# A hybrid decoder layer on one core: expert routing and the last chunk's normalisation rearranged

## The reference

```python
y = mixer(x, ...)
x = layer_norm(ALPHA * x + y, ln1_w, ln1_b)
y = moe(x, router_w, router_b, w_gate, w_up, w_down)
x = layer_norm(ALPHA * x + y, ln2_w, ln2_b)

def moe(x, ...):
    s = sigmoid(x @ router_w)                       # 1024 tokens x 16 experts
    sel = s + router_b
    # the group (of 4 experts) with the greatest sum of its two best sel wins;
    # the two best experts of that group are taken
    gate = s of the two / their sum
    out = sum over e of combine[:, e] * ((silu(x @ w_gate[e]) * (x @ w_up[e])) @ w_down[e])
```

## Time and profile before

| | us |
|---|---|
| median of 3 runs (lowest, highest) | 1000.78 (1000.57, 1002.73) |
| the profiled execution's own time | 1001.21 |
| its span | 999.5 |
| TensorE busy in it | 909.5 |
| VectorE busy | 646.9 |
| ScalarE busy | 447.3 |
| GpSimd busy | 193.7 |
| mean granted TensorE clock | 0.956 of full |

### The profile page before, as it was taken

One profiled execution on the slowest core, in us unless ns is written; L12 is line 12 of the kernel. 1 busy time (PEld: TensorE's weight loads), 2 busy tenths in 40 slices (PEclk: granted clock), 3 DMA queues, 4 the chain that ended last, 5 costly groups with the idle time before them and its releaser, 6 DMA issues.

```text
span 999.5 us, 15243 instructions
## 1 busy us (share of the span) xinstructions
PE 909.5 (91%) x5056; PEld 781.3 (78%) x5056; DVE 646.9 (65%) x985; ACT 447.3 (45%) x586; POOL 193.7 (19%) x192
## 2 busy tenths in 40 slices
PE   6999999999985989998249999999999999999936
PEld 6998887888764878887249889898898988988911
DVE  3442699894236687785682668577689975243766
ACT  3531101102157334411423678576789966255513
POOL 3100011011121121100021322332234422214310
PEclk9999999999996999999559999999999999999969
DMA  7620213133516255312765869979699997648254
GB/s 280 214 90 1 95 52 127 55 125 107 179 63 209 81 184 168 121 64 106 294 206 182 307 201 365 357 249 372 185 373 392 393 373 266 188 120 258 43 183 174
DMA packets 70116, 194.91 MB, mean 195 GB/s; under 512 B 6990, under 2 KB 20640, under 8 KB 70080
## 3 DMA queue, kind: packets, MB, share of 16 engines
q1 hardware_dynamic: 58896, 156.36, 42.7%
q0 software_dynamic: 11040, 37.95, 14.0%
q10 hardware_dynamic: 144, 0.14, 0.0%
HBM read 158.75 MB, written 35.67 MB: 195 GB/s over the span
## 4 chain that ended last, share of the span: by engine, by line
PE 82%; DVE 9%; issue 5%; DMA 2%; ACT 1%; DVEq 0%; SPq 0%; POOL 0%; ACTq 0%; POOLq 0%
PE banks L1109 18%; PE banks L623 14%; PE banks L612 13%; PE banks L637 13%; PE banks L1106 9%; PE banks L1223 6%; PE banks L596 2%; PE banks L1244 2%; PE banks L603 1%; DVE arena L897 1%; DVE small L893 1%; PE banks L1090 1%; DMA sum_scratch<-work,tile_sums 1%; PE banks L1158 1%; DMA arena<-in_x 1%
## 5 line engine op out<-in xcount | busy, mean ns | idle before, releaser
L832 DVE TENSOR_TENSOR split_weights<-arena,split_weights 128x1024 fp32r<-128x1024 f32 x192 | 223.2, 1217 | 0.0
L670 ACT ACTIVATE split_weights<-arena 128x1024 fp32r<-128x1024 f32 x192 | 191.4, 1057 | 3.3 <-DMA arena<-in_w_up 1.8
L1109 PE MATMUL banks<-split_weights 128*128 128x512 f32 (+2 forms) x960 | 181.8, 350 | 0.0
L1109 PEld LDWEIGHTS banks<-split_weights 128*128 128x128 f32 x960 | 155.5, 190 | 23.9 <-issue 1.4
L623 PE MATMUL banks<-split_weights,split_rows 128*128 128x256 f32 x1152 | 147.5, 284 | 0.0
L623 PEld LDWEIGHTS banks<-split_weights,split_rows 128*128 128x128 f32 x1152 | 142.7, 191 | 1.9
L612 PE MATMUL banks<-split_weights,split_rows 128*128 128x512 f32 x576 | 137.4, 395 | 5.5 <-DVE split_rows L836 5.5
L637 PE MATMUL banks<-split_weights,split_hidden 128*128 128x512 f32 x576 | 137.5, 394 | 0.0
L612 PEld LDWEIGHTS banks<-split_weights,split_rows 128*128 128x128 f32 x576 | 110.1, 191 | 29.0 <-issue 5.9
L637 PEld LDWEIGHTS banks<-split_weights,split_hidden 128*128 128x128 f32 x576 | 106.5, 188 | 21.6
L554 POOL DMA_INDIRECT sum_scratch<-work,tile_sums x24 | 90.6, 3775 | 117.3 <-ACT work L707 105.0
(11 more groups left out here) (312 smaller groups left out, 996.2 us busy)
## 6 DMA issues: line engine op xcount, KB each, us to landing
arena<-in_w_gate SPq DMA_DIRECT2D x64, 512.0 KB, 7.7
arena<-in_w_up SPq DMA_DIRECT2D x64, 512.0 KB, 8.4
arena<-in_w_down SPq DMA_DIRECT2D x64, 512.0 KB, 10.4
arena<-in_w_in SPq DMA_DIRECT2D x20, 512.0 KB, 5.4
arena<-in_x SPq DMA_DIRECT2D x16, 512.0 KB, 6.3
arena<-in_w_out SPq DMA_DIRECT2D x8, 512.0 KB, 4.6
x_scratch<-arena SPq DMA_DIRECT2D x8, 512.0 KB, 2.9
sum_scratch<-arena SPq DMA_DIRECT2D x8, 512.0 KB, 4.4
```

The lines of the kernel that those rows point to most:

```text
L670: act.activation(unit_split(u, 0), unit_slot(u), AF.Copy).then_inc(xw_hi, 1)
L832: dve.tensor_tensor(unit_split(u, 1), unit_slot(u), unit_split(u, 0).bitcast(F32), ALU.subtract).then_inc(xw_lo, 1)
L1109: last = pe.matmul(b[:, 0:width], xT[:, hx, k, j * P:(j + 1) * P], wc[:, hw, k, 0:width], start=(k == 0 and i == 0), stop=(k == KC - 1 and ...
```

## The change

1. **Normalisation.** Statistics of a chunk's first half are taken one step earlier. The two passes `norm1` and the product with the weight become one centring pass (mean and weight, no square root needed) and one pass that scales and adds the bias. For the last chunk this second pass, the transposes of x1, their copy and the routing run in two halves. The x1 transposes read contiguous columns, and the router's weights are loaded in the order to match (pieces of 64 B instead of 512 B).
2. **First tile.** A short way gives its tokens: tile 0 holds expert 0's first 128 tokens, so the rank alone places them; a 128x1024 one-hot and 8 products of two columns give the token indices, and the gather of tile 0 starts at once. Its rows are transposed, copied and subtracted in halves. The list of all tokens is summed after that.
3. **Gates.** Normalised gates of all tokens and experts (64 B a token) are stored to DRAM once. For each tile GpSimd gathers the rows of its tokens, and ScalarE's scale is that row's column of the expert. Gate parts, gate one-hots and gate sums are gone.
4. **Weights.** Units 0 to 3 of the first expert are loaded in step 6 and split in steps 8 (2, 3) and 9 (0, 1); units 4 to 7 are loaded in step 7. The other units are split behind the rows. Two small constants are made in step 8.
5. Tile counts have a signal of their own, on which each engine waits before it reads them. In step 9 chunk 6's logits are read after the last chunk's centring pass. The final sums' loads use the staging semaphores.

```diff
 def sp_experts(sp):
-    sp.wait_ge(hT_ps, T)
-    for u in range(8):
-        load_unit(sp, 0, u)
...
+    sp.wait_ge(gates_ready, 1)
+    sp.dma_start(gate_dram[P:P + SEQ, :].rearrange("(t p) e -> p t e", p=P), rt[:, 2]).then_inc(gates_out, 16)
...
+    def gather_gates(j, first=False):
+
+        if not first:
+            pool.wait_ge(gate_in, 16 * j)
+        pool.tensor_copy(tok_gate, tok[:, bass.ds(j, 1)]).then_inc(gate_idx_ready, 1)
+        wait_apart(pool, gate_idx_ready, j + 1)
+        pool.indirect_dma_start(out=gate_rows, out_offset=None, in_=gate_dram,
+                                in_offset=bass.IndirectOffsetOnAxis(ap=tok_gate, axis=0)).then_inc(gate_in, 16)
...
+        if more or not last:
+            gather_gates(g + 1)
...
+    pool.wait_ge(first_tok_ready, 1)
+    pool.indirect_dma_start(out=xe, out_offset=None, in_=x1_dram,
+                            in_offset=bass.IndirectOffsetOnAxis(ap=tok1, axis=0)).then_inc(xe_in, 16)
     pool.wait_ge(tok_ready, 1)
-    gather(0, True)
     gather(1)
+    pool.wait_ge(gates_out, 16)
+    gather_gates(0, True)
     for i, src in enumerate((ln2_w[0], ln2_b[0])):
...
+    pe.wait_ge(first_hot_ready, 1)
+    for t in range(T):
+        last = pe.matmul(bank(3)[:, 0:2], hot_first[:, t, :], first_ids[:, t, :], start=(t == 0), stop=(t == T - 1))
+    last.then_inc(first_ps, 1)
...
+    pe.wait_ge(xe_in, 16)
+    for k in range(KC):
+        last = pe.transpose(psum[:, 4 + k // 4, (k % 4) * P:(k % 4 + 1) * P], xe[:, k:D:KC], ident[:, :])
+        if k == KC // 2 - 1:
+            last.then_inc(first_T, 1)
...
+    pe.wait_ge(ntiles_ready, 1)
+    pe.wait_ge(xw_lo, 4)
...
-    for u in range(8):
+    for u in range(4, UNITS):
...
+    for half, transposed, signal in ((0, first_T, first_hi), (1, xeT_ps, xe_hi)):
+        act.wait_ge(transposed, 1)
+        act.activation(XR[:, 0, half * 4:half * 4 + 4, :], bank(4 + half).rearrange("p (k n) -> p k n", n=P), AF.Copy).then_inc(signal, 1)
...
+        act.wait_ge(gate_in, g * 16 + 16)
         act.activation(ys, psum[:, 2:4, :].rearrange("p a n -> p (a n)"), AF.Copy,
-                       scale=gate_slot[:, bass.ds(g, 1)]).then_inc(y_sb, 1)
+                       scale=gate_rows[:, bass.ds(e, 1)]).then_inc(y_sb, 1)
...
-    dve.tensor_copy(ones_bf, ones[:, :])
-    dve.tensor_tensor(stri, tri[:, :], ident[:, :], ALU.subtract)
...
+    dve.wait_ge(dispatch_ready, 1)
+    own.link(dve.tensor_scalar(others, disp[:, :, 0], -1024.0, 1024.0, ALU.mult, ALU.add))
+    dve.tensor_copy(first_ids[:, :, 0], i_tok.to_broadcast([P, T]))
+    dve.tensor_copy(first_ids[:, :, 1], i_lo[:, 1:T + 1])
...
+    own.link(dve.tensor_tensor(first_key, bank(0)[:, 0:T * NE].rearrange("p (t e) -> p t e", t=T)[:, :, 0], others, ALU.add))
+    dve.tensor_tensor(hot_first, i_lo.unsqueeze(1).to_broadcast([P, T, P]), over(first_key, P), ALU.is_equal).then_inc(first_hot_ready, 1)
     own.link(dve.tensor_copy(cnt[:, 0, :], bank(1)[:, 0:NE]))
+    dve.wait_ge(first_ps, 1)
+    own.link(dve.tensor_copy(first_sum, bank(3)[:, 0:2]))
+    dve.scalar_tensor_tensor(tok1, first_sum[:, 1:2], float(P), first_sum[:, 0:1], ALU.mult, ALU.add).then_inc(first_tok_ready, 1)
+
+    own.link(dve.tensor_tensor(rtv(2), rtv(0), disp, ALU.mult))
+    own.link(dve.tensor_reduce(mx, rtv(2), AX.X, ALU.add))
+    own.link(dve.reciprocal(mx, mx))
+    dve.scalar_tensor_tensor(rtv(2), rtv(2), 1.0 / ALPHA, over(mx, NE), ALU.mult, ALU.mult).then_inc(gates_ready, 1)
...
-    dve.tensor_copy(ntiles[0:1, 0:2], packed_sum)
-    dve.tensor_scalar(ntiles[0:1, 2:3], cnt[0:1, 3, NE - 1:NE], 1.0 / P, None, ALU.mult)
+    dve.tensor_copy(ntiles[0:1, 0:2], packed_sum).then_inc(ntiles_ready, 1)
...
+    for half, copied, signal in ((0, first_hi, first_lo), (1, xe_hi, xe_lo)):
+        dve.wait_ge(copied, 1)
+        dve.tensor_tensor(XR[:, 1, half * 4:half * 4 + 4, :], bank(4 + half).rearrange("p (k n) -> p k n", n=P),
+                          XR[:, 0, half * 4:half * 4 + 4, :].bitcast(F32), ALU.subtract).then_inc(signal, 1)
...
-    of_both(gatew, 0)
...
-    for i in range(3):
-        last = dve.tensor_tensor(hot_gate[:, :, i * 32:(i + 1) * 32], hot_tile,
-                                 gate_parts[:, i].unsqueeze(2).to_broadcast([P, 2 * T, 32]), ALU.mult)
-    last.then_inc(gate_hot_ready, 1)
...
-    for u in range(2):
+    for u in range(4, UNITS):
         split_lo(0, u)
-    dve.wait_ge(gate_sums_ps, 1)
-    own.link(dve.tensor_copy(gate_sum, bank(3)[:, 0:96]))
...
-    dve.tensor_tensor(gate_slot, gate_sum[:, 0:32], gate_sum[:, 32:64], ALU.add).then_inc(gates_ready, 1)
-    for u in range(2, 6):
-        split_lo(0, u)
-    rows_lo(0)
-    for u in range(6, UNITS):
-        split_lo(0, u)
+    dve.wait_ge(ntiles_ready, 1)
...
+        if ch.n == T - 2:
+            sp.wait_ge(w_lo, 28 + KC)
+            for u in range(4):
+                load_unit(sp, 0, u)
+        if ch.n == T - 1:
+            sp.wait_ge(hT_ps, T)
+            for u in range(4, 8):
+                load_unit(sp, 0, u)
...
-    sp.dma_start(rw, router_w.rearrange("(p k) e -> p k e", k=KC)).then_inc(ln1_in, 16)
+    sp.dma_start(rw, router_w.rearrange("(k p) e -> p k e", p=P)).then_inc(ln1_in, 16)
...
+        else:
+            pe.wait_ge(x1_half, 1)
...
+            if ch.n == T - 1 and k == KC // 2:
+                last.then_inc(x1T_half_ps, 1)
+                pe.wait_ge(x1_ready, T)
...
+        if ch.n == T - 1:
+            act.wait_ge(x1T_half_ps, 1)
+            act.wait_ge(lg_ps, PRIMED + ch.c)
+            act.activation(x1T[:, 0:512], bank(2), AF.Copy).then_inc(x1T_half, 1)
+            act.wait_ge(x1T_ps, PRIMED + ch.c + 1)
+            act.activation(x1T[:, 512:D], bank(3), AF.Copy).then_inc(x1T_sb, 1)
...
+        if n == T + 1:
+            act.wait_ge(y_half, 2 * T)
+            for u in (0, 1):
+                expert_hi(act, 0, u, None)
         if n >= 2:
             deviation(rs_c, mv_c[:, 1:2], LN_EPS, r_stats, ch.c - 1, r_std)
+        if n == T:
+            for u in (2, 3):
+                expert_hi(act, 0, u, None)
...
+    def half_statistics1(ch, half):
+        dve.wait_ge(y_summed, 2 * ch.c + half + 1)
+        return dve.bn_stats(st_c[:, half, :], xin[ch.b][:, half * 512:half * 512 + 512])
...
+        wait_apart(dve, dve_own, own.done(half_statistics1(ch, 1)))
...
+    def centre1(ch):
+        v = xin[ch.b]
+        dve.wait_ge(ln1_in, 48)
+        dve.wait_ge(r_stats, ch.c + 1)
+        dve.scalar_tensor_tensor(v, v, mv_c[:, 0:1], ln1[:, 0, :], ALU.subtract, ALU.mult)
...
-        own.link(dve.tensor_scalar(v, v, mv_c[:, 0:1], rs_c, ALU.subtract, ALU.mult))
...
-        own.link(dve.tensor_tensor(v, v, ln1[:, 0, :], ALU.mult))
...
-        dve.tensor_tensor(x1s, v, ln1[:, 1, :], ALU.add).then_inc(x1_ready, 1)
+        if ch.n < T - 1:
+            dve.scalar_tensor_tensor(x1s, v, rs_c, ln1[:, 1, :], ALU.mult, ALU.add).then_inc(x1_ready, 1)
+        else:
+            for half, signal in ((slice(0, 512), x1_half), (slice(512, D), x1_ready)):
+                dve.scalar_tensor_tensor(x1s[:, half], v[:, half], rs_c, ln1[:, 1, half], ALU.mult, ALU.add).then_inc(signal, 1)
...
-            norm1(ch.plus(-2))
+            centre1(ch.plus(-2))
+        if n == T + 1:
+            read_logits(ch.plus(-3))
...
             residual1(ch.plus(-1), 0)
+            half_statistics1(ch.plus(-1), 0)
...
+        if n == T:
+            dve.tensor_copy(ones_bf, ones[:, :])
+            dve.tensor_tensor(stri, tri[:, :], ident[:, :], ALU.subtract)
+            for i, u in enumerate((2, 3)):
+                expert_lo(dve, 0, u, i + 1)
+        if n == T + 1:
+            for i, u in enumerate((0, 1)):
+                expert_lo(dve, 0, u, i + 3)
+        if norms and n != T:
             read_logits(ch.plus(-2))
```

More of the change, by code:

```diff
@@ L229, in hybrid_kernel @@
         slot = sm(2, T)
-        gatew = sm(2, T)
         st_a = sm(T, 6)
@@ L533, in pool_experts, with gather @@
         def pool_experts(pool, own):
[L534 to L537 removed]
+            def gather(j):
+                pool.wait_ge(xe_in, 16 * j)
                 pool.tensor_copy(tok1, tok[:, bass.ds(j, 1)]).then_inc(idx_ready, 1)
[L539 to L544 removed]
+                pool.wait_ge(xeT_ps, j)
+                wait_apart(pool, idx_ready, j)
                 pool.indirect_dma_start(out=xe, out_offset=None, in_=x1_dram,
                                         in_offset=bass.IndirectOffsetOnAxis(ap=tok1, axis=0)).then_inc(xe_in, 16)
+            def gather_gates(j, first=False):
[5 more added lines that the diff above has]
+                                        in_offset=bass.IndirectOffsetOnAxis(ap=tok_gate, axis=0)).then_inc(gate_in, 16)
             def add_rows(g):
@@ L586, in pe_experts @@
             last.then_inc(rank_ps, 1)
-            pe.wait_ge(hot_ready, 1)
-            for i in range(2 * T):
-                last = pe.matmul(bank(2)[:, 0:64], hot_lo[:, i, :], hot_hi[:, i, :], start=(i == 0), stop=(i == 2 * T - 1))
```

(5 more changed lines are left out.)

103 lines of the change are left out of this document (46 added, 57 removed).

## The result

The changed kernel takes 985.54 us, median of four runs (984.71 to 987.97), against 1001.08 for the kernel before beside it: ratio 0.984, 95% interval 0.982 to 0.986. The forecast was 982.1. The profiled run took 985.54 with a span of 983.8; before, 999.5. So 15.7 us of span have gone, where 18.7 were forecast.

The account below looks back on a forecast made before the run. TensorE was taken as the bound, 82% of the chain, with waits for VectorE to cut: 4.0 + 5.0 + 9.7 = 18.7 us off 1001.21 gives 982.5 profiled, 982.1 for the median; range 977.8 to 987.3.

Parts of the forecast that it names:

- the conditions that the forecast itself set: Wrong if low parts wait for the gather, tiles exceed 18.04 with scaling waiting, or a loop step stays near 20.
- Part 1: Chunk loop: VectorE reaches the scores 1.6 us earlier, steps drop to 19.17 us; gain 4.0 us, bounds 2.0 and 4.5.
- Part 2: Last chunk up to its logits: normalisation and routing in halves, at half clock, end at 478.75 instead of 483.79; gain 5.0 us.
- rival a: Last chunk: the clock stays up across the shorter pause, 2.7 us more gain, 979.4; chance 0.17.
- Part 3: Ranks to first product: short way for tile 0, VectorE ends the wait, product at 506.95 instead of 516.62; gain 9.7 us.
- The gather is the other bound: Tile 0's gather: 4.35 us assumed; amid weight loads 7.2 median, 9.5 at most, which slips the start 2.5 to 3 us.
- unseen, I take 0: Before the first product: TensorE's reading of the tile counts costs 0, bounds 0 and 2 us.
- rival b: First product waits for a gather of 7 to 9.5 us or the counts' reading; costs 1.5 to 4 us; chance 0.15.
- Part 4: Every tile: one more gather, of gate rows, 2 us of GpSimd issue; 0 for all tiles.
- rival c: Tight tiles: gate rows land late, 4.3 us a tile, 39 us in nine, 1021; chance 0.08.
- 1 us sooner or later: First tile: when it gets its clock back; this allowance widens the lower end of the range a little.

Follow-up runs that it names:

- a_again: The changed kernel, unedited, run and profiled once more: 987.51 us, ratio 0.9850 to the kernel before.
- hold_loads: Changed kernel, with expert 1's loads started only when the rows of tile 0 have landed: 988.68 us, ratio 0.9870 to the kernel before.
- early_counts: Changed kernel, with tile counts computed early and read by TensorE before it waits for the gathered rows: 986.12 us, ratio 0.9834 to the kernel before.
- hold_counts: Changed kernel, with expert 1's loads held for tile 0's rows and tile counts read early: 985.01 us, ratio 0.9834 to the kernel before.
- norm_only: Kernel before, with only the new normalisation, the last chunk's halves and the later logits' read: 996.25 us, ratio 0.9937 to the kernel before.
- long_way: Changed kernel with the first tile's short way undone, its tokens taken from the full list: 995.25 us, ratio 0.9936 to the kernel before.
- late_split: Changed kernel, with units 0 to 3 of expert 0's gate weights split in the experts' stage again: 988.00 us, ratio 0.9854 to the kernel before.
- gates_twice: Changed kernel, with each tile's gate rows fetched twice, the second time into an unread buffer: 985.07 us, ratio 0.9826 to the kernel before.
- route_mid: Changed kernel, with the logits' 16 thin products between the out projection's last product groups in loop steps: 980.11 us, ratio 0.9767 to the kernel before.
- pause_back: Changed kernel, with two more VectorE statistics passes before the weighted scores in every loop step: 988.90 us, ratio 0.9863 to the kernel before.

## Why the forecast was right, and where it was not

**Direction and most of the size were right**, and 985.5 lies inside the range of 977.8 to 987.3. That it does is in part luck: the unforecast 2.8 us of tile 0, less the 0.8 of the final part, make up for 2.0 us, and without them 987.5 would lie just outside; a_again measured 987.51. By two of the conditions that the forecast itself set it was wrong in its details: the low parts did wait for the gather, and two loop steps took 20.8 us. The failing steps are these.

**Part 1, "so those steps drop to TensorE's own pace: 60.46 - 3 x 19.17".** The mechanism was right: VectorE no longer holds the transposes of h, and undisturbed steps take 19.17 us. The step that failed is the silent one that the pace is reached at a granted clock of 1.00, as in the earlier trace rows. A dip costs 1.65 us, two to four of them take 3.3 to 6.6 of a gain of 4.0. Over the nine profiles with the new normalisation and no further edit of the loop (changed, a_again, hold_loads, early_counts, hold_counts, norm_only, long_way, late_split, gates_twice) the last loop step starts at 442.1 on average, 440.1 to 444.9, against 441.6 before. In the changed kernel's profile the end of the last out projection came 0.64 us earlier, outside the forecast's bounds of 2.0 to 4.5; over the nine profiles the first part was worth nothing in the loop.

**Part 2, 5.0 us.** 5.2 in the changed kernel, 5.6 in norm_only. The choice of the half clock was right too; rival a didn't occur in any of these profiles.

**Part 3, 9.7 us**, came to 7.7. Its terms up to the tokens of tile 0 add up to 2.55 us, not to the 2.45 of its 496.3, and 2.3 were measured. The chain named was right, VectorE through the slots' work to the low parts, and hold_counts shows it at 12.7 us (forecast 13.1) once two terms are out of the way. They are the ones set too low: "The gather is the other bound" was set aside for 2 us of slack, but it took 7.2 us instead of 4.35. Expert 1's loads started where the forecast had them, 4.2 us after the ranks (492.07; its 498 stands on the clock of the profile before), and it had said that they meet the gather; the time it took was still that of a gather with nothing beside it. The gather also went out 0.9 us after its index was ready, and so only 0.9 us ahead of the loads. The other term is the reading of the counts, "unseen, I take 0", which costs 1.2. That is rival b, in part, and both of its halves at once, which the forecast had as alternatives. The early splits are worth 1.0 us as the kernel stands (late_split), and they are also what lets expert 1's loads meet the gather.

**Part 4, 0**, is right; rival c, the slower side, is refuted by the row of L736 and by gates_twice. The Trainium skill (GPSIMD Engine Reference, Key points) has GpSimd and VectorE contend for shared SBUF interfaces where two inputs are read, which might have stretched the new issue; L553 never takes over 2.0 us, also beside VectorE's subtractions. Scatters span the same 1.6 to 6.8 us as in the earlier trace rows. But beside the same eight subtractions of the kernel before the scatter at 594.36 took 2.29 us and the one at 630.45 took 6.83, so that these subtractions alone stretch them is not shown. The Trainium skill (DMA: Bandwidth & Descriptors, Specifications) wants pieces of 512 B or more for the full rate; with 128 pieces of 64 B a tile, even twice, no run here shows a cost, as nobody waits for them.

**What made up for it** was not forecast as a gain: tile 0, 2.8 us shorter in the changed kernel's profile. Its 24 gate products take 5.7 us there, in gates_twice and in route_mid, and 7.2 to 8.1 in the others; the two profiles of the kernel before have 8.5 and 7.1. The range allowed 1 us sooner or later for this; it is nearly 3. What brings the clock back sooner in three of the twelve profiles with an edited or changed kernel is not known.

## What to carry to other kernels

When a change brings an engine to its own pace, leave room in the bounds for the lower clock, even where the trace before shows none, and look at which thin instructions and short waits then stand back to back; an order that sets the thin ones between dense ones gave 5 to 7 us here (980.1 against 985.5 and 987.5), as much as the whole new normalisation (norm_only: 0.0063 of 1002, 6.3 us). When two waits end within a microsecond of each other, removing either alone shows next to nothing (0.4 and 0.8 us), both together show the whole (2.3). Work that is moved forward also empties its buffer sooner: ask what transfer starts then, and beside what. Reading a value from memory into an engine's registers is an instruction on the path like any other: place it where that engine waits anyway.

## What the runs showed of the hardware that was not expected

- The granted clock falls to its lower level (1.2 GHz) for 3.4 to 3.5 us at a time amid a loop in which TensorE is 97% busy (18.6 of 19.17 us). In each of ten profiles it fell in two to four steps, from behind the 16-column products and the short wait that follows them; in the two of the kernel before, with the same sequence in steps of 20.1 us, and in the two with the thin products between dense ones, in no step. In pause_back, with undisturbed steps of 20.2 us, it fell in every second step. Why it spares the kernel before stays open; shown is only that one order, which moves the thin products and takes the wait away with them, had no fall in two profiles.
- A gather of 128 rows lands 4.4 to 4.5 us after its issue with an idle DMA, 7.2 to 8.4 us amid weight loads. In late_split, where the loads start later, it is 4.5 again.
- Where TensorE reads two values between its last products and the next, 1.7 to 2.5 us pass, of which the profile says only "issue". In the changed kernel 1.2 us of it come after the operands are ready; with the reading moved ahead of a wait it is 0.13 (early_counts).
